# The items of an attention block in the order B B B C B C, and its squares summed per head by ScalarE

## The reference, cut to what matters

```python
# mixer B: differential attention, 4 heads, two softmaxes per head
logits = einsum('bthmd,bshmd->bhmts', qblk, k) * scale + bias      # m = 0, 1
p = softmax(where(allowed, logits, -inf))
attn = p[:, :, 0] - lam * p[:, :, 1]
o = einsum('bhts,bshe->bthe', attn, v)                              # 128 values per head
o = o * rsqrt(mean(o * o, -1) + 1e-5) * subln_g * (1.0 - lam_init)  # per head

# mixer C: 4 heads of 64, each query sees its 256 best keys
score = sum_h wi * relu(qi . ki);  sel = top_k(score, 256)
o = softmax(q . k[sel] * scale - slope * dist) @ v[sel]
```

## Time and profile before

| | us |
|---|---|
| median of 3 runs | 2200.95 |
| profiled execution, its own time | 2206.01 |
| its span, first to last instruction | 2204.2 |
| TensorE busy in the span | 2114.9 (96%) |
| VectorE busy | 1100.8 (50%) |
| ScalarE busy | 747.2 (34%) |
| attention, first transpose to last `c_out` | 1126.92 to 1347.06 |
| mean granted TensorE clock | 0.977 of full |

### The profile page before, as it was taken

The page is one execution under the profiler, slowest core; times in us unless marked ns, Lnnn a source line. Parts: engine busy times, 40 slices in busy tenths (PEclk is TensorE's granted clock), DMA queues, the critical chain, the costliest instruction groups (busy, mean ns, idle before and its releaser), DMA issues.

```text
span 2204.2 us, 25891 instructions
## 1 busy us (share of the span) xinstructions
PE 2114.9 (96%) x9834; PEld 1698.6 (77%) x9834; DVE 1100.8 (50%) x1720; ACT 747.2 (34%) x1189; POOL 178.0 (8%) x159
## 2 busy tenths in 40 slices
PE   5999999999999999999987898999999999999998
PEld 4888888878888887688855667878788888888877
DVE  7743463663334373867778884473321222222236
ACT  3311124431112443655765654232111112111133
POOL 1000002300000231112200000310000000000000
PEclk6999999999999999999979999999999999999999
DMA  8433333222111422201100002221111111111131
GB/s 299 146 117 95 101 105 94 78 66 68 47 42 52 127 80 86 59 11 39 54 23 1 1 1 103 89 77 48 48 57 45 43 55 48 41 55 54 49 127 77
DMA packets 222092, 154.75 MB, mean 70 GB/s; under 512 B 6565, under 2 KB 209462, under 8 KB 221878
## 3 DMA queue, kind: packets, MB, share of 16 engines
q1 hardware_dynamic: 215392, 134.53, 20.1%
q0 software_dynamic: 4608, 16.78, 2.3%
q10 hardware_dynamic: 2006, 2.31, 0.3%
HBM read 145.21 MB, written 8.39 MB: 70 GB/s over the span
## 4 chain that ended last, share of the span: by engine, by line
PE 85%; DVE 9%; ACT 4%; issue 2%; POOL 1%; ACTq 0%; DMA 0%; DVEq 0%; POOLq 0%; SPq 0%
PE pair L2068 36%; PE pair L2085 18%; PE pair L2518 8%; PE pair L2304 5%; PE pair L2271 3%; PE pair L2126 3%; PE pair L2405 2%; PE pair L2373 2%; PE pair L2588 1%; DVE act_region L1686 1%; PE pair L2387 1%; PE pair L2097 1%; PE pair L2292 1%; ACT proj L983 1%; DVE w_lo L1310 1%
## 5 line engine op out<-in xcount | busy, mean ns | idle before, releaser
L1316 DVE TENSOR_TENSOR w_lo<-w_raw,w_hi 128x1024 fp32r<-128x1024 f32 x101 | 123.8, 1225 | 672.4 <-ACT w_hi L767 672.2
L767 ACT ACTIVATE w_hi<-w_raw 128x1024 fp32r<-128x1024 f32 x102 | 108.2, 1061 | 804.0 <-PE pair L2068 623.1
L2068 PE MATMUL pair<-act_hi,w_hi 128*128 128x512 f32 x1168 | 361.3, 390 | 1.8 <-ACT v_all L923 1.8
L2068 PE MATMUL pair<-act_lo,w_hi 128*128 128x512 f32 x1168 | 359.7, 389 | 0.0
L2068 PE MATMUL pair<-act_hi,w_lo 128*128 128x512 f32 x1168 | 359.5, 389 | 0.0
L2068 PEld LDWEIGHTS pair<-act_hi,w_hi 128*128 128x128 f32 x1168 | 218.9, 188 | 48.8 <-ACT v_all L923 2.2
L2068 PEld LDWEIGHTS pair<-act_lo,w_hi 128*128 128x128 f32 x1168 | 219.2, 188 | 45.7
L2068 PEld LDWEIGHTS pair<-act_hi,w_lo 128*128 128x128 f32 x1168 | 219.2, 188 | 45.6
L2085 PE MATMUL pair<-act_hi,w_hi 128*128 128x512 f32 x608 | 245.8, 404 | 3.7 <-DVE act_lo L1329 2.0
L2085 PE MATMUL pair<-act_hi,w_lo 128*128 128x512 f32 x608 | 239.4, 394 | 0.0
L2085 PE MATMUL pair<-act_lo,w_hi 128*128 128x512 f32 x608 | 239.4, 394 | 0.0
(11 more groups left out here) (406 smaller groups left out, 3166.2 us busy)
## 6 DMA issues: line engine op xcount, KB each, us to landing
w_raw<-w_in SPq DMA_DIRECT2D x76, 512.0 KB, 3.7
w_raw<-w_out SPq DMA_DIRECT2D x48, 512.0 KB, 3.9
w_raw<-w_gu SPq DMA_DIRECT2D x48, 512.0 KB, 3.7
w_raw<-w_down SPq DMA_DIRECT2D x24, 384.0 KB, 3.0
act_region<-w_ada SPq DMA_DIRECT2D x16, 512.0 KB, 13.4
sq<-w_ada POOLq DMA_DIRECT2D x16, 512.0 KB, 4.1
sq_sum<-w_ada POOLq DMA_DIRECT2D x16, 512.0 KB, 4.8
yT<-x SPq DMA_DIRECT2D x8, 512.0 KB, 7.6
```

Source lines behind the costliest of these rows:

```text
L767: A(w_hi[s_][:], w_raw[s_][:], ACT.Copy).then_inc(hi_ready, 1)
L1316: v.tensor_tensor(w_lo[s_][:], w_raw[s_][:], f32(w_hi[s_][:]), ALU.subtract)\
L2068: i = mm(bank[pair][:, h * HALF:(h + 1) * HALF], w[slot][:, k, :], a[:, k, h * HALF:(h + 1) * HALF], start=(k == 0 and w is w_hi and a is ...
```

## The change

The order of a block becomes B0 B1 B2 C0 B3 C1. The squares of the B results are now taken head by head, each with a sum that ScalarE writes to `o_ss`, so `ob_squares` on VectorE is gone. Squares and copy move from p4 to p5, since B3 is now at p4. `c_low` moves from the end of VectorE's step p3 to its start, ahead of `biased(k+1)`. The row sums `den` keep their old places through `den_of`. The rest is index arithmetic.

```diff
+ITEM_ORDER = (0, 1, 2, 4, 3, 5)
+AFTER_B = ITEM_ORDER.index(BH - 1) + 1
+def kind(item):
+    return item // ITEMS, ITEM_ORDER[item % ITEMS]
 def groups_of(item):
-    return 1 if item % ITEMS < BH else 2
+    return 1 if kind(item)[1] < BH else 2
+def b_rank(item):
+    return sum(kind(n)[1] < BH for n in range(item))
...
 # ScalarE
-                if it == BH:
+                if it == AFTER_B:
                     act.wait_ge(pv_done, group(k - 1, 0) + 1)
-                    if i:
-                        act.wait_ge(ob_sum, i)
-                    A(junk[:], bank[3][:, 0:HALF], ACT.Square).then_inc(ob_sq, 1)
+                    act.wait_ge(ob_sq, BH * i)
+                    for h in range(BH):
+                        A(junk[:, h * BV:(h + 1) * BV], bank[3][:, h * BV:(h + 1) * BV], ACT.Square,
+                          accum_out=o_ss[:, i, h:h + 1]).then_inc(ob_sq, 1)
                     A(o_nat(i), bank[3][:, 0:HALF]..., ACT.Copy).then_inc(ob_taken, 1)
...
 # VectorE
             for k in range(N_ITEMS):
                 i, it = divmod(k, ITEMS)
+                if i and it == 3:
+                    c_low(i - 1)
                 if k + 1 < N_ITEMS:
                     biased(k + 1)
-                if it < BH:
+                if kind(k)[1] < BH:
                     combine(k)
...
-                if i and it == 3:
-                    c_low(i - 1)
-                if it == 5:
-                    ob_squares(i)
...
 # TensorE
             def turn(item, k):
-                if item % ITEMS < BH:
-                    pe.wait_ge(attn_ready, i * BH + item % ITEMS + 1)
+                if kind(item)[1] < BH:
+                    pe.wait_ge(attn_ready, b_rank(item) + 1)
```

More of the change, by code:

```diff
@@ L121, in pairs_of, with at_kind @@
     return [q for q in range(len(PPS)) if PPS[q][0] == item]
+def kind(item):
+    return item // ITEMS, ITEM_ORDER[item % ITEMS]
 def groups_of(item):
-    return 1 if item % ITEMS < BH else 2
+    return 1 if kind(item)[1] < BH else 2
+def b_rank(item):
+    return sum(kind(n)[1] < BH for n in range(item))
+def at_kind(i, it):
+    return i * ITEMS + ITEM_ORDER.index(it)
 def group(item, k):
@@ L434, in tiles, with den_of @@
             return slice(a * TT // 2, (a + 1) * TT // 2)
+        def den_of(item):
+            i, it = kind(item)
+            return den[:, i * ITEMS + it, :]
         def staged(t):
@@ L1036, in exps @@
                       bias=neg_max[:, item % 3, m, n > HALF:(n > HALF) + 1],
-                      accum_out=den[:, item, m:m + 1]).then_inc(exp_done, 1)
+                      accum_out=den_of(item)[:, m:m + 1]).then_inc(exp_done, 1)
             def turned(item, k):
@@ L1673, in biased @@
             def biased(item):
-                i, it = divmod(item, ITEMS)
+                i, it = kind(item)
                 if item >= 3:
@@ L1696, in combine @@
                 dve.wait_ge(exp_done, 2 * item + 2)
-                own.did(v.reciprocal(den_r[:, 0:1], den[:, item, 1:2]))
-                own.did(v.scalar_tensor_tensor(den_r[:, 1:2], den[:, item, 0:1], den_r[:, 0:1], lam[:, 0:1],
+                own.did(v.reciprocal(den_r[:, 0:1], den_of(item)[:, 1:2]))
+                own.did(v.scalar_tensor_tensor(den_r[:, 1:2], den_of(item)[:, 0:1], den_r[:, 0:1], lam[:, 0:1],
                                                ALU.mult, ALU.mult))
@@ L1704, in c_out @@
                 k = i * ITEMS + BH
-                dve.wait_ge(pv_done, group(k + 1, 1) + 1)
+                dve.wait_ge(pv_done, group(at_kind(i, BH + 1), 1) + 1)
                 own.did(v.reciprocal(c_den[:], den[:, k:k + 2, :].rearrange("p a m -> p (a m)")))
@@ L1716, in c_low @@
                                 ALU.subtract).then_inc(c_lo, 1)
[L1718 to L1721, removed]
             def ob_variance(a):
-                dve.wait_ge(ob_sum, 4 * a + 4)
+                dve.wait_ge(ob_sq, BH * (4 * a + 4))
                 ss, od = o_ss[:, tiles(a)], o_den[:, tiles(a), :]
```

## The result

The changed kernel takes **2211.08 us** (median of 5 runs, 2210.69 to 2216.74) against 2200.95 for the kernel before (5 runs beside it, 2200.27 to 2204.13). The ratio is 1.0052, 95% interval 1.0042 to 1.0063: **slower by 0.5%**, 10.1 us. The forecast was 2209.5, +8.5 us.

A forecast was written before the change was run, and what follows sets the result against it. The bound was taken to be the order in which TensorE and VectorE wait for each other. Blocks and tail +2.2 us, clock +6.3, together +8.5 on the median 2200.95: 2209.5 us, range 2200.5 to 2214.0.

The forecast's parts named there:

- The round trip: Blocks 4 to 7, p3: TensorE's logits wait through ScalarE's `c_hi` and VectorE's `c_low`; +3.3 us in block 7.
- The idle time before `c_low`: VectorE at p3 stands waiting for ScalarE's `c_hi`: 0.9 us in block 6, more in block 7.
- The single blocks, without the clock: Blocks 0 to 7: changes in time from order, placing and squares at unchanged clock, summing with the tail to +2.2 us.
- block 7's tail: End of block 7: C0 now at p3, where second logits fill one of three waits, -1.2 us.
- Blocks 0 to 3: Short blocks: +0.3, +0.2, -0.2 and +0.6 us, the last three from ScalarE's copy at p3 behind later exponentials.
- The clock: TensorE behind the new waits in blocks 4 to 7: four dips to the lower clock, 1.58 us each, +6.3 us.
- rival 3: Another exposed dip in block 4 at p2 (+1.6) and Squares without overlap (+2): 2213 us; chance 0.10.
- Rival 1: Blocks 4 to 7: round trip there but TensorE's clock holds, +2.2 us, 2203.2; chance 0.22 with up to two dips.
- Rival 2: ScalarE early enough that `c_low` doesn't wait, so the interleaving pays: -3.8 us, no dips, 2197.2; chance 0.13.
- dear squares: ScalarE's four Squares without overlap add 0.5 us in each of four short blocks, +2 us.
- Rival 4: The squares were the point: VectorE's 0.69 us a block worth 5.5 us in eight blocks, 2195.5; chance 0.02.
- That dips cost nothing before: Kernel before, TensorE's waits of 2.94 and 2.29 us: the lower clock behind them was hidden, VectorE being later.

The follow-up runs named there:

- `c_hi` early: The changed kernel with `c_hi` taken on ScalarE at the end of p1 instead of p2, `c_low` still ahead of `biased`: 2199.88 us, ratio 0.9991.
- the filled kernel: The changed kernel plus 12 useless TensorE products between the transposes of p2 and the logits of p5 in blocks 4 to 7: 2206.05 us, ratio 1.0025.
- the first experiment: The changed kernel with `c_low` at p3 put back behind `biased`, new order and new squares kept: 2197.14 us, ratio 0.9979.
- the change without the squares: The changed kernel with the old squares: one Square of 512 on ScalarE and VectorE's sum per head, now at p0: 2214.90 us, ratio 1.0067.
- 24 fillings: The changed kernel plus 24 useless TensorE products between the transposes of p2 and the logits of p5, blocks 4 to 7: 2215.58 us, ratio 1.0062.
- the order alone: The new order of items with the old squares and `c_low` behind `biased`, against the kernel before: 2196.29 us, ratio 0.9978.
- the squares alone: The kernel before with only the four Squares with sums on ScalarE and no sum on VectorE: 2202.49 us, ratio 1.0007.
- the kernel before with its waits filled: The kernel before plus 7 useless TensorE products inside each of its waits at p2 of blocks 4 to 6: 2203.94 us, ratio 0.9998.

## Why the prediction was right

**The round trip** was the step that mattered. It was worked out at 4.13 us from transposes to logits in block 7, and measured 4.16; in block 6 at 3.92 (1284.58 to 1288.50), and measured 4.02 (1288.30 to 1292.32). The idle time before `c_low` in block 6 was forecast at 0.9 us and measured 1.23. Three edits that take it away by different means (`c_low` behind, `c_hi` early, both) each take the loss away, and the old order with this placing alone loses 0.8%. That is shown. At the full clock the placing alone is worth +3.3 us in block 7, as forecast: 37.84 us in the filled kernel, 34.52 in the first experiment.

**The single blocks, without the clock.** Blocks 5 to 7 of the filled kernel stand for the change with a full clock. Block 7 is there 1.9 us longer than before (37.84 against 35.91), forecast 3.3 - 1.2 = 2.1. Of the three waits of block 7's tail (the earlier trace rows has one) two are left, 1.11 and 1.20 us, as forecast. Block 6: +0.5 (39.66 against 39.16), forecast 0.0. Block 5: +0.9, forecast -0.1. Block 4: its +2.6 less two dips gives -0.5, forecast -0.7. Blocks 0 to 3 were the worst: forecast +0.9 together, measured -1.3. The forecast had looked there for what the placing delays and not for what the order saves, and the first experiment tells the two apart. With `c_low` behind, blocks 1 to 3 are 1.1, 1.3 and 0.7 us shorter than before; the change gives 0.8, 0.6 and 0.4 of it back. It does so by the mechanism that was forecast, for its waits before the transposes that ScalarE's copy at p3 ends are 1.77, 1.27 and 1.17 us, against 0.59, 0.67 and 0.78 with `c_low` behind. (In block 1 a part is clock: it is low until 1149 in the profile before and until 1146 in the one after.) All blocks together: +1.5 against a forecast of +2.2.

**The clock** was forecast at four dips of 1.58 us, 6.3. Measured in the profiled execution were five, of about 8.9 us. That is 2.6, 1.6 and 1.6 in blocks 5 to 7 from the comparison above, and in block 4 1.55 behind the wait of 2.10 us: from these logits to those of p5 it is 7.92 us (1209.43 to 1217.35), and 6.37 in the change without the squares, where no dip followed. The fifth is taken at 1.6 like the two it resembles. 1.5 + 8.9 = 10.4, the 10.36 measured. This agreement confirms nothing, for in blocks 4 to 7 each part was found as what the other leaves of the measured difference; what supports the split is that the change without the squares gives the same prices in blocks 5 and 7 (38.88 - 36.33 = 2.55 and 39.40 - 37.84 = 1.56). The term that was off is thus the clock's, by the number of dips: I had counted the wait of 2.10 us as safe, from one row of one execution (1245.23), and put the dip of block 4 in rival 3 alone. The dip in block 5 was also a longer one than the one I had measured. The two errors, 2.6 us too little clock and 0.7 too much elsewhere, partly cancel, and to that extent the close total (+8.5 against +10.1) is luck. The profiled execution itself was forecast at 2214.5 and took 2210.87, by the -1.3 and -4.2 outside the stretch.

**How certain a dip is** can't be said in one number. Behind the 2.10 us of block 4 there was one in the change (both profiles), in the kernel with 12 fillings and with `c_hi` early, and none with 24 fillings, without the squares or with the order alone. The waits themselves repeat to 0.01 us. The change's first five times fall into two groups, near 2210.8 and near 2216.6, with mean clocks of 0.977 and 0.973. (The Trainium skill, "TensorE: Matmul & The Clock Gate", section "What's actually happening", says that the monitor's time base is not tied to the kernel's start. That would fit 0.50 and 1.00 behind the same wait of 2.92 us in two kernels, but the two profiled executions of the change itself had the same five dips, so no trace here shows dips that vary within one program.)

**The rivals.** Rival 1, clock held: the waits were right, the clock wrong; the twelve fillings show most of what it would have been. Rival 2, ScalarE early enough: not so here, 1.23 us of idle time; made true by the earlier `c_hi`, it came out at 2199.88 against its 2197.2. Rival 3: its dip in block 4 happened; its dear squares did not, 1.00 us for four against 1.1 estimated, with no effect. Rival 4: refuted by the squares alone, 1.0007.

**That dips cost nothing before** was argued. By the kernel before with its waits filled it holds for the total, within what could be measured (ratio 0.9998, 0.9989 to 1.0007), but not for block 4, where about 1.0 us of the dip behind the 2.94 us was exposed.

## What to carry to other kernels

A small instruction moved ahead of the one that feeds the busiest engine hands down its whole chain of waits: follow what it waits for back to the engine that you want to keep busy, before you price it by its own 0.4 us. A wait of two or three microseconds on TensorE can cost another 1.6 to 2.6 us in clock, if nothing hides it. Time the parts of such a change one by one: here a good order (-0.2%) came with a bad placing (+0.7%).

## What was not expected

A float32 product of 128x128 by 128 columns took 0.22 us and stands as two records in the profile (12 products, 24 records, 2.84 us; 24 products 5.52, so 2.68 for twelve more). A low clock can begin a microsecond behind the wait: behind 3.07 us in the old order the first product took 0.73 us, as at the full clock, and the next four took 1.93 instead of 1.13. And a wait of 1.83 us was once followed by a dip (0.66, then 0.50 from 1292 to 1294, `c_hi` early), which is shorter than any that I had thought of as costly. Shorter still is the 0.90 us at p1 of block 4 in the two kernels with `c_low` behind and the new squares: behind it the clock fell as well (0.57 from 1202 to 1206 in the first experiment), where the kernel before and the change kept theirs.
